# Stick-breaking attention with both heads of a pair side by side in the array, the mask inside the scan, and part of the convolution moved into the gates' panels

## The reference, cut to what matters

```python
def stick_breaking_attention(q, k, v):
    ...
    for blk in range(S // Q_BLOCK):          # 8 blocks of 128 queries
        ...
        z = jnp.einsum('bthd,bshd->bhts', qb, kb).astype(jnp.float32) * scale
        causal = s_pos < t_pos
        log_fail = jnp.where(causal, jax.nn.log_sigmoid(-z), 0.0)
        later = lax.cumsum(log_fail, axis=3, reverse=True) - log_fail
        w = jnp.where(causal, jnp.exp(jax.nn.log_sigmoid(z) + later), 0.0)
        outs.append(jnp.einsum('bhts,bshd->bthd', w.astype(vb.dtype), vb))

    c = glu_a * jax.nn.sigmoid(glu_b)
    c = causal_depthwise_conv(c, conv_w, conv_b)
    c = jax.nn.silu(layer_norm(c, conv_ln_g, conv_ln_b))
    conv_branch = jnp.einsum('bsc,cd->bsd', c * jax.nn.silu(z_conv), w_conv_proj) + b_conv_proj
    merged = jax.nn.sigmoid(g_att) * att_branch + jax.nn.sigmoid(g_conv) * conv_branch
```

## Time and profile before

| what | value |
|---|---|
| median of 3 runs | 3452.89 us (3452.77 to 3453.93) |
| the profiled execution's own time | 3454.11 us |
| its span in the trace | 3452.3 us |
| mean granted PE clock in it | 0.99 of full speed |
| PE busy | 3366.0 us, 97% |
| DVE busy | 1489.6 us, 43% |
| POOL busy | 1434.2 us, 42% |
| ACT busy | 751.6 us, 22% |
| attention stage, first score to first G_ATT matmul | 2627.8 to 3000.7 us |

### The profile page before, as it was taken

One profiled execution on the slowest core, in us unless ns is written; L12 is line 12 of the kernel. 1 busy time (PEld: TensorE's weight loads), 2 busy tenths in 40 slices (PEclk: granted clock), 3 DMA queues, 4 the chain that ended last, 5 costly groups with the idle time before them and its releaser, 6 DMA issues.

```text
span 3452.3 us, 38334 instructions
## 1 busy us (share of the span) xinstructions
PE 3366.0 (97%) x15180; PEld 2618.5 (76%) x15180; DVE 1489.6 (43%) x2111; ACT 751.6 (22%) x1476; POOL 1434.2 (42%) x1320
## 2 busy tenths in 40 slices
PE   7999999999999999999999999999999999899996
PEld 5776788888888787767888888887876555688875
DVE  5545451212123555554621212134668888614134
ACT  3222230101012321222310101023222334203012
POOL 5632354444444446323544444443544222245541
PEclk9999999999999999999999999999999999999998
DMA  4111221111111221112311111111111000011111
GB/s 142 44 44 42 68 62 49 49 46 48 56 49 49 67 81 44 44 28 83 58 49 49 49 49 55 46 48 52 45 49 31 19 19 19 19 49 43 52 46 67
DMA packets 341746, 173.69 MB, mean 50 GB/s; under 512 B 58048, under 2 KB 334528, under 8 KB 341568
## 3 DMA queue, kind: packets, MB, share of 16 engines
q1 hardware_dynamic: 324592, 162.49, 16.6%
q10 hardware_dynamic: 16976, 8.76, 0.8%
HBM read 155.15 MB, written 12.91 MB: 49 GB/s over the span
## 4 chain that ended last, share of the span: by engine, by line
PE 91%; DVE 6%; ACT 1%; issue 1%; ACTq 0%; DMA 0%; DVEq 0%
PE ring L911 28%; PE ring L913 27%; PE ring L912 27%; PE aux L1146 2%; PE aux L1174 2%; DVE conv_out L1948 1%; PE aux L1010 1%; DVE left L1960 1%; PE aux L986 1%; PE aux L996 1%; DVE rstd L1660 0%; PE aux L1160 0%; PE ring L966 0%; PE aux L1273 0%; PE ring L972 0%
## 5 line engine op out<-in xcount | busy, mean ns | idle before, releaser
L745 POOL TENSOR_TENSOR w_hi<-w_raw,ones 128x512 fp32r<-128x512 f32 (+3 forms) x536 | 567.6, 1059 | 1492.1 <-PE ring L913 1481.6
L911 PE MATMUL ring<-Q_hi,w_hi 128*128 128x512 f32 x1856 | 735.7, 396 | 1.7 <-DVE s_half L1980 1.7
L911 PE MATMUL ring<-P_hi,w_hi 128*128 128x512 f32 x1792 | 721.1, 402 | 8.9 <-DVE pool_u L1676 5.0
L913 PE MATMUL ring<-Q_hi,w_lo 128*128 128x512 f32 x1856 | 725.4, 391 | 0.0
L912 PE MATMUL ring<-Q_lo,w_hi 128*128 128x512 f32 x1856 | 724.7, 390 | 0.0
L913 PE MATMUL ring<-P_hi,w_lo 128*128 128x512 f32 x1792 | 700.5, 391 | 0.0
L912 PE MATMUL ring<-P_lo,w_hi 128*128 128x512 f32 x1792 | 700.3, 391 | 0.0
L747 POOL TENSOR_TENSOR w_lo<-w_raw,w_hi 128x512 fp32r<-128x512 f32 (+3 forms) x536 | 663.2, 1237 | 42.0
L911 PEld LDWEIGHTS ring<-Q_hi,w_hi 128*128 128x128 f32 x1856 | 349.7, 188 | 89.3 <-issue 18.3
L911 PEld LDWEIGHTS ring<-P_hi,w_hi 128*128 128x128 f32 x1792 | 337.5, 188 | 104.0 <-issue 24.1
L913 PEld LDWEIGHTS ring<-Q_hi,w_lo 128*128 128x128 f32 x1856 | 349.6, 188 | 73.8
(11 more groups left out here) (247 smaller groups left out, 3641.7 us busy)
## 6 DMA issues: line engine op xcount, KB each, us to landing
w_raw<-in_w_in SPq DMA_DIRECT2D x84, 512.0 KB, 3.8
w_raw<-in_w_up SPq DMA_DIRECT2D x64, 512.0 KB, 4.0
w_raw<-in_w_down SPq DMA_DIRECT2D x64, 512.0 KB, 4.0
h_scratch<-h ACTq DMA_DIRECT2D x16, 512.0 KB, 2.9
w_raw<-in_w_gate SPq DMA_DIRECT2D x16, 512.0 KB, 4.1
hx<-h_scratch SPq DMA_DIRECT2D x12, 512.0 KB, 6.6
x_raw<-in_x SPq DMA_DIRECT2D x8, 512.0 KB, 7.9
w_raw<-in_w_out SPq DMA_DIRECT2D x16, 256.0 KB, 2.8
```

The source lines that it names most:

```text
L745: g.tensor_tensor(w_hi[:, slot, ks], w_raw[:, slot, ks], one.broadcast_to([P, width, P]), ALU.mult).then_inc(w_hi_ready, 1)
L911: t.matmul(o, wh, xh, start=first, stop=False)
L913: return t.matmul(o, wl, xh, start=False, stop=last)
```

## The change

It works on both heads of a pair in one step. There are 12 rounds to a pair instead of 16 units: query blocks 0 to 3 in one round each, blocks 4 to 7 in two (512 keys, then the rest), 3 chunks apart. In a round the scores of head 0 and head 1 are issued one behind the other, from partitions 0 to 63 and 64 to 127, into two PSUM banks; `meet` takes 256 queries of both heads, alternating between them, into the two halves of the same bank's partitions. The mask matmul goes: the scan combines "times the fail" with "max of 1 on and before the diagonal" from a constant tile `not_yet`, and the weights on the diagonal block are set to 0 by an affine select on POOL (`mask_shares`, 8 per pair, 128x256). A scan of more than 512 elements becomes two, and there are two heads, so DVE issues 24 scans for a pair instead of 16 and 12 products instead of 16. `convolve` behind a round stays only where the round is narrower than 512 keys or has no scan; the 44 taps that are left go into G_ATT, 9 behind each of the first panels' products. The two sums over channels come one panel (pair) later, and the Z_CONV gates are kept in four buffers (`conv_in`, free by then).

```diff
+ROUNDS = [(qb, part, min(HALF, P * (qb + 1) - HALF * part)) for qb in range(8) for part in range(1 + qb // 4)]
+TURN_LAG, MEET_LAG = 2, 3
+STEPS2 = len(ROUNDS) + MEET_LAG
...
-            k = 2 + 5 * u // 2
+            k = 2 + 3 * u
...
+        g.memset(not_yet[:], 0.0).then_inc(keep_made, 1)
+        g.affine_select(out=not_yet[:, 0:P], in_=not_yet[:, 0:P], compare_op=ALU.is_ge, fill=1.0, base=-P, pattern=[[1, P]], channel_multiplier=1)\
+            .then_inc(keep_made, 1)
...
+        def mask_shares(c, r):
+            nth = len(ROUNDS) * c + r
+            pool.wait_ge(z_beta, nth + 1)
+            on_diagonal = weight[:, nth % 2, :, 0:P]
+            g.affine_select(out=on_diagonal, in_=on_diagonal, compare_op=ALU.is_ge, fill=0.0, base=-P, pattern=[[0, 2], [1, P]], channel_multiplier=1)\
+                .then_inc(z_masked, 1)
...
+                    if job[2] < len(ROUNDS) and ROUNDS[job[2]][1] == 0:
+                        mask_shares(*job[1:])
...
+            for kb in range(7, 5 - 2 * g, -1):
+                at = max(0, 7 - kb - 2 * g) * P
+                for e in range(2):
+                    rows = slice(64 * e, 64 * e + 64)
+                    mm = t.matmul(meet_bank[rows, at:256], v2[c % 2][:, kb, rows], weight_t[:, kb, e, at:256],
+                                  start=(kb == 7), stop=True, skip_group_check=True)
...
+            for e in range(2):
+                if nth:
+                    pe.wait_ge(z_taken, 2 * (nth - 1) + e + 1)
+                for i in range(blocks):
+                    mm = t.transpose(turn_banks[e][:, i * P:i * P + P], weight[:, nth % 2, e, i * P:i * P + P], ident[:])
...
-                mm = t.matmul(score_bank[:, at:stop], query, k2[buf][rows, S - n + at:S - n + stop], start=True, stop=True)
-                if at == 0:
-                    mm = t.matmul(score_bank[:, 0:P], ident_r[:], keep_r[:], start=False, stop=True, skip_group_check=True)
+            for e in range(2):
+                rows = slice(64 * e, 64 * e + 64)
+                mm = t.matmul(score_bank[:, e, 0:n], q2[buf][rows, qb * P:qb * P + P], k2[buf][rows, first:first + n], start=True, stop=True)
...
-            if f == 5:
+            if f == 6:
                 ln_sum(stat_sum, LN_MEAN1)
         for f in range(4):
             panel2(Z_CONV + f, Q_hi, Q_lo, None)
-            if f == 0:
+            if f == 1:
                 ln_sum(stat_sum, LN_VAR1)
...
+            if nth >= 2:
+                act.wait_ge(z_scanned, 2 * (nth - 1))
+            a.activation(fail[:, nth % 2, :, 0:n], score_bank[:, :, 0:n], ACT.Sigmoid, scale=-1.0).then_inc(z_failed, 1)
+            a.activation(weight[:, nth % 2, :, 0:n], score_bank[:, :, 0:n], ACT.Sigmoid).then_inc(z_beta, 1)
...
-        gate(Z_CONV, 24, ACT.Silu)
+        for f in range(2):
+            gate(Z_CONV + f, 24 + f, ACT.Silu, conv_in[:, f])
         ln_deviation(2, 512)
...
-            if f >= 1:
-                gate(Z_CONV + f, 24 + f, ACT.Silu)
+            if f >= 2:
+                gate(Z_CONV + f, 24 + f, ACT.Silu, conv_in[:, f])
             branch_high(f)
...
+            for e in range(2):
+                factor, at = fail[:, nth % 2, e, 0:m], HALF * part + 1
+                if part:
+                    v.tensor_tensor_scan(left[:, e, at:at + m], factor, factor, left[:, e, HALF:HALF + 1], ALU.mult, ALU.min).then_inc(z_scanned, 1)
+                else:
+                    v.tensor_tensor_scan(left[:, e, at:at + m], factor, not_yet[:, 0:m], 1.0, ALU.mult, ALU.max).then_inc(z_scanned, 1)
+            dve.wait_ge(z_beta, nth + 1)
+            dve.wait_ge(z_masked, blocks_masked(c, r))
+            dve.wait_ge(z_scanned, 2 * nth + 2)
+            share_of = weight[:, nth % 2, :, 0:n]
+            v.tensor_tensor(share_of, share_of, left[:, :, HALF * part:HALF * part + n], ALU.mult).then_inc(z_weighed, 1)
...
-                        convolve(1)
+                        if job[2] >= len(ROUNDS) or ROUNDS[job[2]][2] < HALF:
+                            convolve(1)
...
+            if f < 5:
+                convolve(9)
+            if f == 5:
+                convolve(len(todo) - taken)
                 dve.wait_ge(convolved, taken)
...
-            if f == 6:
+            if f == 7:
                 centre(conv_out, 4, 512, 1)
```

More of the change, by code:

```diff
@@ L208, with meets_after, blocks_masked @@
 XN_AT = {c: i for i, c in enumerate(c for pair in XN_PAIRS for c in pair)}
[L211 to L215, removed]
+def meets_after(u):
+    r = u - MEET_LAG
+    if 0 <= r and ROUNDS[r][0] % 2 and (r + 1 == len(ROUNDS) or ROUNDS[r + 1][0] != ROUNDS[r][0]):
+        return ROUNDS[r][0] // 2
+    return None
+def blocks_masked(c, r):
+    return 8 * c + ROUNDS[r][0] + 1
 def in_pattern(x, g):
@@ L482, in two_blocks @@
     z_beta = sem("z_beta")
+    z_masked = sem("z_masked")
     z_scanned = sem("z_scanned")
@@ L1135, in turn_v2, with meet @@
             mm.then_inc(v2_turned, 1)
[L1137 to L1141, removed]
+        def meet(c, g):
+            group = 4 * c + g
+            r = max(i for i, (qb, part, n) in enumerate(ROUNDS) if qb == 2 * g + 1)
+            pe.wait_ge(z_taken, 2 * (len(ROUNDS) * c + r + 1))
             if group:
                 pe.wait_ge(att_taken, group)
[L1144 to L1147, removed]
+            for kb in range(7, 5 - 2 * g, -1):
[4 more added lines that the diff above has]
+                                  start=(kb == 7), stop=True, skip_group_check=True)
@@ L1148, in meet, with turn_weights @@
             mm.then_inc(z_met, 1)
[L1150 to L1153, removed]
+        def turn_weights(c, r):
+            nth, blocks = len(ROUNDS) * c + r, ROUNDS[r][2] // P
+            pe.wait_ge(z_weighed, nth + 1)
+            if r == 0:
                 pe.wait_ge(v2_taken, 2 * c + 2)
[L1155 to L1160, removed]
-                mm.then_inc(z_turned, 1)
@@ L1510, in break_sticks, with take_met @@
[L1510 to L1517, removed]
+        def take_met(c, g):
+            act.wait_ge(z_met, 4 * c + g + 1)
+            a.activation(att2[:, c, 256 * g:256 * g + 256], meet_bank[:, 0:256], ACT.Copy).then_inc(att_taken, 1)
@@ new lines, in take_turned, with break_sticks @@
+        def take_turned(c, r):
+            qb, part, n = ROUNDS[r]
+            kb, blocks, at_query = 7 - qb + 4 * part, n // P, qb % 2 * P
+            for e in range(2):
+                act.wait_ge(z_turned, 2 * (len(ROUNDS) * c + r) + e + 1)
+                a.activation(weight_t[:, kb:kb + blocks, e, at_query:at_query + P], turn_banks[e][:, 0:n].rearrange("p (b q) -> p b q", b=blocks), ACT.Copy)\
+                    .then_inc(z_taken, 1)
+        def break_sticks(c, r):
+            nth, n = len(ROUNDS) * c + r, ROUNDS[r][2]
+            act.wait_ge(z_scored, nth + 1)
+            if nth >= 2:
+                act.wait_ge(z_scanned, 2 * (nth - 1))
+            a.activation(fail[:, nth % 2, :, 0:n], score_bank[:, :, 0:n], ACT.Sigmoid, scale=-1.0).then_inc(z_failed, 1)
+            a.activation(weight[:, nth % 2, :, 0:n], score_bank[:, :, 0:n], ACT.Sigmoid).then_inc(z_beta, 1)
```

99 lines of the change are left out of this document (35 added, 64 removed).

## The result

| | time, us | against the kernel before |
|---|---|---|
| before | 3453.41 (3452.77 to 3455.14, 4 runs) | |
| changed | 3393.65 (3391.37 to 3395.72, 4 runs) | 0.9826, interval 0.9812 to 0.984 |

The account below looks back on a forecast made before the run. PE bounded before; DVE would pace after, at 68.5 us per pair. Three pairs save 53.5 us and the last pair 22, less 1.5 behind the attention: 74 off the 3452.89 median, 3379 us, range 3354 to 3410.

Parts of the forecast that it names:

- Scores and masks, meets and transposes: PE per pair: scores 10.1 us, masks nothing, weights by values 7.9, 72 transposes stay; PE would need 64.
- DVE's work: DVE per pair: scans, products, taps and takes 55.4 us, 66 with POOL's part.
- Splits: POOL's splitting of weight panels slows DVE's taps and scans: 8.4 us per pair.
- selects: Eight diagonal masks on POOL cost DVE 2 us per pair, range 0 to 4.
- its early wait: DVE waits for PE early in each pair: 2.5 us, added to its 66 to give 68.5.
- a clock term: In Z_ATT, new waits lower PE's clock: 5 us taken, between 0 and 15.
- The last pair: In Z_ATT, PE waits at ACT's copy and DVE sets the pace: 92 us instead of 113.8.
- the gate of the third panel: Z_CONV gate behind the second branch's copy in ACT's queue; G_CONV about 1.5 us late, between 0 and 5.
- PE as the only bound: Rival: PE bounds every stage, 64 us per pair, Z_ATT 86; 3358 us, chance 0.14.
- Full exclusion of DVE and POOL: Rival: DVE and POOL exclude each other wholly, 75 to 76 us per pair; 3409 us, chance 0.15.
- No overlap: Rival: heads do not overlap in the array at 256 to 512 columns, 82 us per pair; 3436, chance 0.04.
- The clock spiral: Rival: attention waits lower PE's clock, each low stretch making the next; some 3500 us, chance 0.05.

Follow-up runs that it names:

- The later taps: Changed kernel with three convolution taps per pair moved from among the wide rounds to behind them: 3380.82 us, 0.9788.
- the lag: Changed kernel with high and low parts of the gated attention made one half later in Z_ATT, on ACT and DVE: 3384.13 us, 0.9796.

## Why the prediction was right or wrong

- **The bound and its shift.** Right: PE bounded before, DVE paces after. PE's own pair is 64.2 us for 64. Scores and masks, meets and transposes came as costed.
- **DVE's work.** Right within 1 us: 62.85 busy and some 2.2 in its own scan-to-product and product-to-scan waits, 65 for 66. Splits 6.7 for 8.4, selects 2.2 for 2, so the rest is 56.1 for 55.4 (the sum without POOL's part).
- **The pair's length: the step that failed** is "I take DVE's 66 and the 2.5 us of its early wait: 68.5 us per pair". It took DVE as busy from its first fail to the pair's end. DVE also idles 4.0 us before the last take, because the last half holds few rounds, and the taps that could fill it stand ahead of the wide rounds: 65 + 2.5 + 4.0 = 71.5 of the 71.9 us. PE's waits were forecast as four or five of 1 to 2 us; three were 0.28, 0.59 and 1.13, and the fourth was 3.68 and brought the low clock with it, 1.5 us a pair. I had put a clock term on the last pair alone. 3 x (72.25 - 68.5) = 11.2 us, nearly all of the miss in the trace. The later taps, which change only the place of taps, bring the pair to 68.2.
- **The last pair.** 92.9 for 92, and for the reason given: the lag removes the waits for ACT, and 6.0 us with them. The granted clock over it was 0.96, so the clock's share is 95.3 x 0.04 = 3.8 us by estimate, where the forecast took 5 for the new waits.
- **G_ATT and Z_CONV.** Nine taps nearly fill a period and PE never waits in G_ATT (behind nine taps DVE idles 2.76, 2.44, 1.10 and 1.04 us before the product, where before it idled 15.10); the gate of the third panel costs 1.2 us for 1.5.
- **Rivals.** PE as the only bound: no, until DVE is relieved of taps or splits (65.7 and 65.9). Full exclusion of DVE and POOL, as a price: no, 6.7 of 14.7 us. The Trainium skill's sentence in SBUF — State Buffer, summary of rules for kernel authors, is that the second to issue fully blocks. The stretched records of both engines fit it, but what I made of it, that DVE pays the splits' whole time, does not follow: it paid less than half. Where the rest went is not shown. No overlap: no, two heads' 512 keys take 1.06 us and the last meet 3.46. The clock spiral: no. The clock fell behind each 3.7 us wait (0.52 to 0.55 over 3.4 us), was at 0.97 to 1.00 over the 3.2 us behind that, and no low stretch made the next.
- **Signs.** As forecast: score rows of four records with 1.06 us to the next start, no mask matmul, one short wait before G_CONV. Not as forecast: DVE was busy 87% of the pair and not over 90%, it waited at the pair's end too, the clock was 0.98 and not 1.00, and a select took 0.77 us in the mean and not 0.5.
- The two traces are 62.4 us apart and the medians 59.8; this 2.6 us is in no step of the prediction.

## What to carry to other kernels

When the bounding engine is relieved, compare the next engine's work with the new length not only in sum but stretch by stretch: here 65 us of work fitted into 68, and took 72 because fill-in work stood before the dense stretch and not behind it. Fill-in work belongs where the engine would wait for the other one, and a queue that holds work for others should not stand behind a late copy. Matmuls of half the array should be issued side by side: with eight transposes between them the two heads' scores took 1.06 us each, and in blocks of one head the meets kept only 0.6 to 0.7 us of overlap.

## What the runs showed of the hardware that was not expected

Meets in the order "all of head 0, then all of head 1" still overlapped in part. At 1.72 ns per column and 0.2 us to start, the four would take 1.5, 3.3, 5.0 and 6.8 us one after the other; they took 0.88, 2.65, 4.38 and 6.10, each 0.6 to 0.7 less. The last two fp32 matmuls of head 0, four records of 256 and 128 columns, are 384 columns or 0.66 us. So head 1 seems to start while up to four records of head 0 are still to run; this is inferred from the sums. The first block's eight records in 0.59 us, four of head 0 and then four of head 1, fit: there it is all of them. This reading rests on five lengths; no run varied the depth.
